# The later modulation blocks multiplied and summed on VectorE instead of TensorE, in a two-layer transformer kernel on one core

## The reference

```python
sc, scc = silu(c), silu(c_ctx)
shift, scale, gate       = split(sc  @ w_ada[l] + b_ada[l], 3)
shift_c, scale_c, gate_c = split(scc @ w_ada[l] + b_ada[l], 3)
h  = rms(x,  norm_w[l]) * (1 + scale)   + shift
hc = rms(xc, norm_w[l]) * (1 + scale_c) + shift_c
u  = h @ w_in[l]            # and hc @ w_in[l]: q, k, v of three attentions, z
x  = x + gate * ((attention outputs * silu(z)) @ w_out[l])
```

## Time and profile before

| | |
|---|---|
| median of 3 runs | 4086.47 us (4072.94 to 4087.55) |
| profiled execution, its own time | 4103.53 us |
| span in the profile | 4101.8 us |
| busy: PE, DVE, ACT, POOL | 3780.7, 1721.4, 1646.2, 67.9 us |
| mean granted TensorE clock | 0.963 of full speed |
| loaded from HBM | 570 MB, 139 GB/s over the span |

### The profile page before, as it was taken

How to read it: one execution, slowest core, us unless ns; L and a number is a source line. 1 busy time by engine, 2 the same in 40 slices (tenths; PEclk the granted TensorE clock), 3 DMA queues, 4 the chain that set the end, 5 groups by cost and what they waited for, 6 DMA issues and landing times.

```text
span 4101.8 us, 46314 instructions
## 1 busy us (share of the span) xinstructions
PE 3780.7 (92%) x19088; PEld 2938.3 (72%) x19088; DVE 1721.4 (42%) x2657; ACT 1646.2 (40%) x2577; POOL 67.9 (2%) x118
## 2 busy tenths in 40 slices
PE   7889999987989889999798999999999879999997
PEld 1557777775766657777666777776777669999886
DVE  1323444222232433443244454444554456666444
ACT  2313344443221323345444434444454554555443
POOL 1100000000010000000000000000000000000000
PEclk8899999998999999999989999999999989999999
DMA  9652221113556454222246555643645436666564
GB/s 360 173 163 67 62 57 47 46 36 97 170 174 182 136 164 134 67 79 66 56 127 197 159 160 169 189 134 112 203 147 175 134 116 188 186 186 188 175 200 149
DMA packets 350738, 577.49 MB, mean 141 GB/s; under 512 B 25268, under 2 KB 131012, under 8 KB 348352
## 3 DMA queue, kind: packets, MB, share of 16 engines
q1 hardware_dynamic: 344208, 549.47, 43.7%
q0 software_dynamic: 6320, 25.06, 2.2%
HBM read 570.26 MB, written 4.19 MB: 140 GB/s over the span
## 4 chain that ended last, share of the span: by engine, by line
PE 56%; DVE 4%; ACT 3%; DMA 1%; issue 1%; ACTq 0%; DVEq 0%
PE ps L680 35%; PE ps L1386 12%; PE ps L1107 2%; DVE w_lo L656 1%; ACT w_hi L650 1%; DMA raw_ring<-in_w_in_dram 1%; PE ps L1021 1%; PE ps L1000 1%; PE ps L1279 1%; PE ps L1286 1%; PE ps L1008 1%; ACT f_arena L1432 0%; PE ps L785 0%; PE ps L706 0%; PE ps L994 0%
## 5 line engine op out<-in xcount | busy, mean ns | idle before, releaser
L656 DVE TENSOR_TENSOR w_lo<-raw_ring,w_hi 128x1024 fp32r<-128x1024 f32 (+1 forms) x827 | 1006.2, 1223 | 1354.2 <-ACT w_hi L650 1353.2
L650 ACT CAST w_hi<-raw_ring 128x1024 fp32r<-128x1024 f32 (+1 forms) x827 | 860.7, 1047 | 1396.1 <-PE ps L680 603.6
L680 PE MATMUL ps<-w_hi,r_a 128*128 128x512 f32 x3552 | 1301.8, 407 | 102.8 <-DVE w_lo L656 36.8
L680 PE MATMUL ps<-w_lo,r_a 128*128 128x512 f32 x2624 | 1042.6, 397 | 0.0
L680 PEld LDWEIGHTS ps<-w_hi,r_a 128*128 128x128 f32 x3552 | 680.1, 191 | 331.7 <-issue 123.1
L680 PE MATMUL ps<-w_hi,r_b 128*128 128x512 f32 x2272 | 865.3, 400 | 11.4 <-DVE w_lo L656 5.5
L680 PEld LDWEIGHTS ps<-w_lo,r_a 128*128 128x128 f32 x2624 | 504.0, 192 | 106.1 <-issue 3.6
L680 PEld LDWEIGHTS ps<-w_hi,r_b 128*128 128x128 f32 x2272 | 436.6, 192 | 115.9 <-DVE w_lo L656 12.6
L1386 PE MATMUL ps<-r_a,w_hi 128*128 128x256 f32 x2816 | 499.8, 282 | 3.0 <-DVE w_lo L656 3.0
L1386 PEld LDWEIGHTS ps<-r_a,w_hi 128*128 128x128 f32 x2816 | 431.6, 189 | 3.1 <-issue 3.1
L1386 PE MATMUL ps<-r_a,w_lo 128*128 128x256 f32 x1408 | 396.6, 282 | 0.0
(11 more groups left out here) (301 smaller groups left out, 2897.7 us busy)
## 6 DMA issues: line engine op xcount, KB each, us to landing
raw_ring<-in_w_in_dram SPq DMA_DIRECT2D x386, 512.0 KB, 3.7
raw_ring<-in_ffn_w_up_dram SPq DMA_DIRECT2D x176, 512.0 KB, 4.4
raw_ring<-in_w_ada_dram SPq DMA_DIRECT2D x128, 512.0 KB, 4.4
raw_ring<-in_w_out_dram SPq DMA_DIRECT2D x96, 512.0 KB, 3.8
raw_ring<-in_ffn_w_down_dram SPq DMA_DIRECT2D x88, 512.0 KB, 3.7
gla_arena<-in_w_ada_dram SPq DMA_DIRECT2D x64, 512.0 KB, 9.0
raw_ring<-in_w_proj_b_dram SPq DMA_DIRECT2D x32, 512.0 KB, 3.7
raw_ring<-in_w_proj_a_dram SPq DMA_DIRECT2D x16, 512.0 KB, 3.7
```

Of the source, the lines that this page charges most:

```text
L650: nc.scalar.copy(WH[:, ph.s_slot(i, j), 0:n], RAW[:, ph.raw_slot(i, j), 0:n]).then_inc(hi_ready, 1)
L656: nc.vector.tensor_tensor(WL[:, ph.raw_slot(i, j), 0:n], RAW[:, ph.raw_slot(i, j), 0:n], WH[:, ph.s_slot(i, j), 0:n].bitcast(F32), ALU.sub ...
L680: mm = nc.tensor.matmul(PS[:, t, 0:cols], X(x, k, t), W[w][:, kk * cols:(kk + 1) * cols], start=(k == 0 and q == 0), stop=(c == len(js) - ...
```

## The change

The 128 later modulation chunks become a kind of their own ("M") and are no longer multiplied by TensorE. VectorE multiplies each half of a chunk (128 by 512) with the condition value of its row and adds it to an accumulator in SBUF: `dve_ada`, one instruction for each half and stream, 4 a chunk, and 2 for the four blocks of layer 1 whose context gate nobody uses (`streams`). The second half waits for the first by a semaphore. When a block's eight chunks are summed, TensorE sums over the partitions with `pe_ada_sum`: 4 products with a column of ones for each stream, 8 or 4 in place of the 4 of `pe_ada_turn`, placed in the middle of the next main chunk. The copy out of PSUM (L738) is gone, the bias stays.

The chunks are also spread anew. `PLACES` gives exactly one to each main chunk of: `win0` block 0 from chunk 2 to block 5 chunk 1; blocks 1 to 3 of `z0`; `wout0` whole; blocks 1 to 4 of `win1`. So 18 of them in layer 0, and 16 in layer 1, now lie in the attention steps. A ring slot of a modulation chunk is given back by VectorE (`mod_used`).

```diff
-        ADAW = U[0:ADAM, 0, CQ + 256:CQ + 768]
+
+        ACC = {"win": U[:, 0:2, CQ + 256:CQ + 768], "z": U[:, 2:4, CKV:CKV + NB],
+               "wout": F[:, E0 + 7168:E0 + 8192].rearrange("p (s n) -> p s n", s=2)}
...
-        HOST = {("win0", 0): ("wide", 8), ("win0", 1): ("double", 9), ("win0", 2): ("front", 11),
-                ("z0", 1): ("double", 12), ("z0", 2): ("wide", 14), ("z0", 3): ("wide", 15),
-                ("wout0", 0): ("wide", 16), ("wout0", 1): ("double", 17), ("wout0", 2): ("wide", 19),
-                ("wout0", 3): ("wide", 20), ("win1", 1): ("double", 21), ("win1", 2): ("front", 23)}
-
-        TURN = {}
-        for (name, b), (how, n) in HOST.items():
-            if how == "wide":
-                TURN[name, b + 1, 1] = n
-            else:
-                TURN[name, b, 5] = n
-                if how == "double":
-                    TURN[name, b + 1, 1] = n + 1
+        PLACES = ([("win0", 0, c) for c in range(2, 8)] + [("win0", b, c) for b in range(1, 5) for c in range(8)]
+                  + [("win0", 5, c) for c in range(2)] + [("z0", b, c) for b in range(1, 4) for c in range(8)]
+                  + [("wout0", b, c) for b in range(4) for c in range(8)]
+                  + [("win1", b, c) for b in range(1, 5) for c in range(8)])
+        HOSTED, TURN = {}, {}
+        assert len(PLACES) == 8 * len(ADAQ)
+        for k, p in enumerate(PLACES):
+            HOSTED.setdefault(p, []).append((8 + k // 8, k % 8))
+            if k % 8 == 7:
+                TURN[p] = 8 + k // 8
 
         def hosted(name, b, c):
 
-            how, n = HOST.get((name, b), ("", 0))
-            if how == "wide" and c % 2:
-                return [(n, c - 1), (n, c)]
-            if how == "double" or how == "front" and c < 4:
-                return [(n + c // 4, 2 * (c % 4)), (n + c // 4, 2 * (c % 4) + 1)]
-            return []
+            return HOSTED.get((name, b, c), [])
+
+        def turned_at(name, b, c):
+
+            return TURN.get((name, b, c - 1) if c else (name, b - 1, 7))
+
+        def streams(n):
+
+            return 1 if n >= 8 and ADAQ[n - 8][0] == 1 and ADAQ[n - 8][1] >= 8 else 2
...
-                    sp.wait_ge(pair_used if k == "S" else plain_used, n + 1)
+                    sp.wait_ge({"S": pair_used, "P": plain_used, "M": mod_used}[k], n + 1)
...
+        def pe_with_sum(pe, name, l, b, c, T):
+
+            ph, st, n = PH[f"{name}{l}"], AC[f"{name}{l}"][b], turned_at(f"{name}{l}", b, c)
+            if n is None:
+                pe_part(pe, ph, b, S8, c, 2, NB, x1, T, st, 0, T)
+            else:
+                pe_part(pe, ph, b, S8, c, 2, NB, x1, T, st, 0, T // 2)
+                pe_ada_sum(pe, n, ACC[name])
+                pe_part(pe, ph, b, S8, c, 2, NB, x1, T, st, T // 2, T)
...
+        def pe_ada_sum(pe, n, acc, to=ADAP):
+
+            pe.wait_ge(mod_used, PH[f"ada{ADAQ[n - 8][0]}"].p(n, 7) + 1)
+            for f in range(4):
+                for st in range(streams(n)):
+                    mm = nc.tensor.matmul(to[:, f, st:st + 1], acc[:, st, f * P:f * P + P], ONE,
+                                          start=True, stop=True)
+            mm.then_inc(ada_tr, 1)
+
+        def dve_ada(dve, n, ci, acc, halves=(0, 1)):
+
+            ph = PH[f"ada{ADAQ[n - 8][0]}"]
+            w = RAW[:, ph.raw_slot(n, ci)]
+            done = ph.p(n, ci)
+            for kk in halves:
+                if kk == 0:
+                    dve.wait_ge(raw_full[ph.raw_slot(n, ci)], ph.raw_full(n, ci))
+                    if ci:
+                        dve.wait_ge(mod_used, done)
+                k = 2 * ci + kk
+                for st in range(streams(n)):
+                    wk = w[:, kk * NB:(kk + 1) * NB]
+                    if k == 0:
+                        ins = nc.vector.tensor_scalar(acc[:, st, :], wk, SCT[:, k, st:st + 1], None, ALU.mult)
+                    else:
+                        ins = nc.vector.scalar_tensor_tensor(acc[:, st, :], wk, SCT[:, k, st:st + 1], acc[:, st, :],
+                                                             ALU.mult, ALU.add)
+                if kk == 0:
+                    ins.then_inc(mod_half, 1)
+                    dve.wait_ge(mod_half, done + 1)
+                else:
+                    ins.then_inc(mod_used, 1)
...
+                    halves = [(n, ci, kk) for n, ci in hosted(f"win{l}", b, c) for kk in range(2)]
+                    size = len(halves) * 2 // WT[l][b]
+                    mods[b, c, lo] = halves[size * (lo // 2):size * (lo // 2) + size]
...
-                        pe_block_part(pe, ph, b, S8, c, 2, NB, x1, range(WT[l][b]), AC[f"win{l}"][b])
-                        if (f"win{l}", b, c) in TURN:
-                            pe_ada_turn(pe, TURN[f"win{l}", b, c], ADAW)
+                        pe_with_sum(pe, "win", l, b, c, WT[l][b])
...
+                    if step in turns:
+                        pe.wait_ge(o_evac, un + before)
+                        pe_ada_sum(pe, turns[step], ACC["win"], ADAV)
                     if before is not None:
                         values(before)
...
+                def mods(name, b, c):
+
+                    n = turned_at(name, b, c)
+                    if n is not None:
+                        dve_ada_bias(dve, n)
+                    for n, ci in hosted(name, b, c):
+                        dve_ada(dve, n, ci, ACC[name[:-1]])
...
+                    mods(win, b, c)
                     rest(q + 2)
                     if c == 7 and b != 2:
...
                 def weights(name, b, c, lo, hi):
+                    if name == "win":
+                        for n, ci, kk in halves[b, c, lo]:
+                            dve_ada(dve, n, ci, ACC["win"], (kk,))
                     if name != "kt" and lo == 0:
```

More of the change, by code:

```diff
@@ L132, in build @@
         SEL = place("ada_sel", 2)
+        ONE = place("one", 1)
         NM = place("neg_max", 2)
@@ L219, in build @@
         PH, seq, kinds = {}, [], []
-        count = dict(S=0, P=0)
+        count = dict(S=0, P=0, M=0)
         def phase(name, iters, chunks):
@@ L885, in ab_parts, with ab_mods @@
             return out
+        def ab_mods(l):
+            steps, parts = ab_steps(l), ab_parts(l)
+            mods = {}
+            turns, end = {}, None
+            for k, step in enumerate(parts):
+                has = k >= 2 and steps[k - 2][0] == "s"
+                if end is not None and has:
+                    turns[k], end = end, None
+                for name, b, c, lo, hi in step:
+                    if name != "win":
+                        continue
+                    halves = [(n, ci, kk) for n, ci in hosted(f"win{l}", b, c) for kk in range(2)]
+                    size = len(halves) * 2 // WT[l][b]
+                    mods[b, c, lo] = halves[size * (lo // 2):size * (lo // 2) + size]
+                    assert not (end is not None and mods[b, c, lo]), (l, b, c)
+                    if hi == WT[l][b] and (f"win{l}", b, c) in TURN:
+                        end = TURN[f"win{l}", b, c]
+            assert end is None
+            return mods, turns
         def chain(l):
@@ L1063, in weights @@
                         pe_part(pe, PH[f"z{l}"], 0, S8, c, 2, NB, x1, T, AC[f"z{l}"][0], lo, hi)
+                turns = ab_mods(l)[1]
                 last = before = None
-                for (what, x), parts in zip(ab_steps(l), ab_parts(l)):
+                for step, ((what, x), parts) in enumerate(zip(ab_steps(l), ab_parts(l))):
                     if what == "s":
@@ L1143, in _ @@
                     for c in range(8):
[L1144 to L1148, removed]
+                        pe_with_sum(pe, "z", l, b, c, T)
                 if l == 0:
-                    pe_ada_turn(pe, 15)
+                    pe_ada_sum(pe, TURN["z0", 3, 7], ACC["z"])
                     pe.wait_ge(ada_free, 16)
@@ L1166, in _ @@
                                 pe.wait_ge(tr_free, y0 + 2)
-                            pe_block_part(pe, ph, i, S8, c, 2, NB, x1, range(4), AC["wout0"][i])
+                            pe_with_sum(pe, "wout", 0, i, c, 4)
                             if i == 0:
@@ L1173, in _ @@
                                 flip(1, c)
-                            if ("wout0", i, c) in TURN:
-                                pe_ada_turn(pe, TURN["wout0", i, c])
-                            for n, ci in hosted("wout0", i, c):
-                                pe_ada(pe, n, ci)
-                    pe_ada_turn(pe, 20)
-                    pe.wait_ge(ada_free, 21)
+                    pe_ada_sum(pe, TURN["wout0", 3, 7], ACC["wout"])
+                    pe.wait_ge(ada_free, 20)
                 else:
@@ L2185, in _ @@
                         u_sums(b)
+                if l:
+                    dve_ada_bias(dve, TURN["win1", 2, 7])
                 units, un = ab_units(l), UN[f"a{l}"]
@@ L2274, in weights @@
                             z_evac(0)
+                halves, turns = ab_mods(l)
                 last = before = None
```

(5 more changed lines are left out.)

51 lines of the change are left out of this document (18 added, 33 removed).

## The result

The changed kernel takes **4056.13 us** (median of 5 runs, 4048.44 to 4060.93) against 4080.85 for the kernel before (5 runs, 4072.94 to 4087.55): a ratio of **0.9919, 95% interval 0.9892 to 0.9946**. It is faster, by 25 us where 112 were forecast, and outside the range of 3940 to 4030. A second set of five runs on another chip gave 4048.71 against 4087.48, ratio 0.9907 [0.9892, 0.9923].

A forecast was written before the change was run, and what follows sets the result against it. The prediction took TensorE, busy 92%, as the bound, with load waits in "double" blocks. Gains of 144 less 10 for lags and 22 for attention steps made 112 us, 4086.5 to 3974 for the median, range 3940 to 4030.

The forecast's parts named there:

- attention steps: Both layers' steps with 34 hosted chunks: late loads, delayed turns and sums cost 22 us, from above 85.
- lags at flips and gates: Dense blocks: 10 us taken off the gain for lags that the 1.5 us of slack there doesn't cover.
- each new time is 8 x 5.51 = 44.1: Dense blocks: eight chunks of 24 matmuls at 0.23 us make 44.1 us, plus the boundary and the block's sum.
- the prediction's rivals: Attention steps lose much more (0.14), VectorE paces dense blocks (0.04), slower (0.04), waits not lifted (0.06), more gain (0.06).
- dense blocks: Hosting blocks of `win0`, `z0`, `wout0`, `win1`: gain 144 us together, 65 of TensorE time inside, some 79 of waits.
- "double" places: Blocks of 82.8, 67.2, 68.9 and 70.3 us, TensorE idle waiting for loads: to shrink to 48 to 55.
- The sums: TensorE's new one-column products per modulation block: 12 at 1.6 us and 4 at 0.8, 22 us in all.
- my upper bound for one sum: A sum on TensorE takes at most 3 us, with low clock and a restart of the main matmuls.
- roughly 0.7 us for two chunks: Layer 0's attention steps: TensorE's loss from turns delayed by late loads, 6 us in all.
- The large version of this rival: Attention steps lose 2 to 2.5 us a chunk, 70 to 85 in all, giving 4020 to 4046; chance 0.14.
- VectorE's price: New products take about 2.8 us a chunk, 1.4 with one stream; about 300 us more busy time, hidden behind TensorE.
- the rule of halved throughput: Rival: doubled instruction times, 5.4 us of VectorE a chunk, pace the dense blocks: 4075 to 4100; chance 0.04.

The follow-up runs named there:

- e9: e1's kernel once more, unedited, one execution: 4027.1 us, with the up projection's 256-column matmuls at 117.8 ns.
- e0: The changed kernel again, unedited, on the second chip, later tiles moved by 32 bytes: 4048.71 us against 4087.48 for the kernel before, ratio 0.9907.
- e2: The kernel before with only 32 bytes of unused space where the change has its column of ones: 4129.26 us, ratio 1.0107 to the kernel before.
- e1: The changed kernel with the column of ones in unused words of an existing tile, so nothing moves: 4001.90 us, ratio 0.9794 to the kernel before.
- e5: e1 with the 34 attention-step chunks loaded, but VectorE multiplying only 8 of 512 columns of each half: 3996.62 us, ratio 0.9778 to the kernel before.
- e6: e1 with the 34 attention-step chunks not loaded, VectorE doing all their products on a constant area: 3985.60 us, ratio 0.9745 to the kernel before.
- e8: The kernel before once more, unedited, one execution: 4083.53 us, with the up projection's 256-column matmuls at 113.3 ns.

## Why the prediction was off

Leads at the boundaries give each stage's gain. The kernel after and e9 are compared with the first profile of the kernel before; all three ran the up projection at about 118 ns:

| stage | forecast | kernel after | e9 (nothing moved) |
|---|---|---|---|
| `win0` blocks 0 to 2 | +51 | +39.3 | +39.8 |
| attention steps, layer 0 | -12 | -22.4 | -20.5 |
| per-head phase, layer 0 | 0 | -8.1 | +0.4 |
| `z0` blocks 1 to 3 | +26 | +21.8 | +22.1 |
| `wout0` | +36 | +20.0 | +22.4 |
| `win1` block 0 | 0 | +3.0 | +3.0 |
| `win1` blocks 1 and 2 | +31 | +30.7 | +30.1 |
| attention steps, layer 1 | -10 | -12.4 | -13.6 |
| per-head phase, layer 1 | 0 | -7.0 | -5.5 |
| all later work | 0 | -17.5 | -1.8 |
| lags at flips and gates | -10 | in the rows | in the rows |
| sum | +112 | +47.4 | +76.5 |

**The step that failed** is the unspoken one behind "each new time is 8 x 5.51 = 44.1" and behind everything that the sum left out: that matmuls which the change doesn't touch keep their pace. They lost 1.7% of it to the 32 bytes of the new tile. Between e0 and e9 this is 20.9 us of span. Between the kernel after and e9 it is 29.1, but 8.5 of them are the per-head phase of layer 0, which varies by execution (below); 15.7 lie in "all later work", where nothing was edited: 4704 main matmuls by 3.9 ns are 18.3. Where a stage waits for loads the slower pace costs little: e2, the kernel before shifted, loses nothing up to the end of layer 1's attention steps (0.2 us behind) and only 15.2 us in all by its profile. The cost of the shift is thus 15 to 21 us by spans. By medians it is more, 42 us between e2 and the kernel before and 47 between e0 and e1, since the unshifted kernels have executions with the better `up` pace in them and no shifted one showed it. That carries the result out of the range: on one chip the change with nothing moved gained 85.6 us by medians (e1), the change as made 38.8 (e0). None of the prediction's rivals had this mechanism in it.

It isn't the whole miss. Of the 64.6 us between 112 and 47.4, e9 accounts for 35.5 with every tile at its old address: 16.6 in the dense blocks, 12.1 in the attention steps, 5.1 in the per-head phases and 1.8 later. These terms were mis-sized, as follows.

**The dense blocks** (134 after the 10 for lags; 117.4 in e9, 114.8 in the kernel after) had the right mechanism. Main chunks in "double" places mostly run at their 5.60 us with their low part 3.0 to 3.6 us early (forecast 3.2), and 1.24 in flip and gate blocks (1.5). What was undersized is what surrounds the boundaries, and the flips (0.85 us a chunk where 0.6 was forecast). TensorE's waits at the boundary ahead of `wout0` block 3, first in the kernel before, then after; two windows of the kernel after, over the first chunk of block 2 and then over the boundary ahead of block 3; and TensorE's timeline in the first chunk of block 3:

```profile
PE ps L680 <- DVE f_arena L2358: 2.4, 1, 2.4
```

```profile
PE ps L684 <- DVE f_arena L2424: 6.1, 1, 6.1
```

```profile
1245.50:1255.70 10.20, 10.18 (x41) 8.35 (x42) 3.76 (x6) 1.05 (x1) 0.73 (x1) 0.75 0.22 84
1300.60:1307.60 7.00, 0.89 (x4) 0.09 (x2) 6.03 (x9) 1.04 (x1) 0.00 (x0) 0.84 0.52 172
```

```profile
1307.58 0.77 PE L684 MATMUL ps<-w_hi,r_a 128*128 128x512 f32 x1 [6.11 <-DVE f_arena L2424]
...
1311.56 0.63 PE L684 MATMUL ps<-w_hi,r_a 128*128 128x512 f32 x1
1311.99 0.46 PE L684 MATMUL ps<-w_lo,r_a 128*128 128x512 f32 x1
1312.29 0.40 PE L684 MATMUL ps<-w_hi,r_b 128*128 128x512 f32 x1
1312.52 1.84 PE L749 MATMUL ps<-one,f_arena 128*128 128x1 f32 x16
```

The evacuation stands behind a flip and a chunk's products on VectorE, and TensorE idles for 6.1 us instead of 2.4. Its next chunk takes 9.52 us where it was 5.60 in the kernel before. Of these 3.9 us, 2.1 are the lower clock: the first eleven matmuls are 0.43 apart (1307.58 to 1312.29) instead of 0.23. The rest is the sum of the modulation block, which stands in this chunk. The prediction priced the boundary and the sum, but slow matmuls after a pause only at the start of `win0` and of `z0`. So block 2 of `wout0` (62.1 for 56.2) is six chunks of 6.45, a first one of 10.25 and a last one, with the pause in it, of 13.13. Block 2 of `win0` (61.9 for 52.5) has a last chunk of 12.75: its boundary took 6.3 us, 4.1 of them idle, and I had costed 2.3. It also has the chunk around its sum, which follows.

**The sums** themselves were sized a little low (twelve of 1.84 to 2.38 us and four of 0.95 to 1.02, against 1.6 and 0.8). A timeline of TensorE in the kernel after, block 2 of `win0`:

```profile
236.84 0.39 PE L684 MATMUL ps<-w_hi,r_b 128*128 128x512 f32 x1
238.00 1.95 PE L749 MATMUL ps<-one,f_arena 128*128 128x1 f32 x16 [0.78 <-DVE f_arena L769]
239.81 0.48 PE L684 MATMUL ps<-w_hi,r_a 128*128 128x512 f32 x1
...
242.07 0.63 PE L684 MATMUL ps<-w_hi,r_a 128*128 128x512 f32 x1
242.50 0.63 PE L684 MATMUL ps<-w_lo,r_a 128*128 128x512 f32 x1
```

The sum is 1.95 us here, but it waits 0.78 for VectorE first, and the matmuls soon after it start 0.43 apart and not 0.23: the lower clock again. The whole chunk took 10.80 us where its neighbours with a flip took 6.45, 4.35 more, above the 3 us of my upper bound for one sum.

**The attention steps** cost 34.1 us (e9) where 22 were forecast. The mechanism was as given (late load, ScalarE and VectorE standing behind it, a delayed turn), and e5 and e6 bear it out; the size, "roughly 0.7 us for two chunks", was small. It left out that TensorE, once it idles, comes back at the lower clock, which is some 8 of the 21 us in e1. ScalarE's wait was 2.8 us a chunk. TensorE lost some 1 us a chunk of it. The large version of this rival, 70 to 85, did not come.

**VectorE's price** was right: 747 ns and 287 us in all, against the 692 to 747 ns of the earlier trace rows and "about 300". On the rule of halved throughput (the Trainium skill, "Vector Engine (DVE) Microarchitecture Reference", "Points that are easy to get wrong"), doubled times of 1.4 us don't appear: a plain `tensor_tensor` of 128x512 with two SBUF sources took 693 ns in the kernel before, the new instruction 747. This trace disagrees with the rule as I had applied it.

**Left open.** By what path an address that is no multiple of 64 bytes slows a matmul, and which of the moved tiles does it, wasn't tried. Nor was what sets the up projection's pace at its start. Shifting by 64 gives 227 to 230 ns for 512 columns and 120.0 for 256, so 64-byte alignment isn't the whole rule. The per-head phase of layer 0 lost 8.1 us in the kernel after, but also in e8, the unedited kernel before, and none in e9: it varies by execution, and I put no cause to it.

The best version is e1, the change with nothing moved: 2.1% faster than the kernel before by its median of four (a later single execution, e9, 1.5% below the one of the kernel before beside it, 4087.03 us), where the change as made is 0.8 to 0.9%.

## What to carry to other kernels

A new tile, however small, is a change to every tile behind it: before a sum of times is trusted, list which addresses move, and compare the pitch of matmuls that nobody edited. Hidden work on an in-order engine is hidden only while that engine's other inputs are early; here 18 chunks of products, some 50 us, cost nothing that could be seen while the loads were early, and about 10 us more than the late loads did alone. And spacing can be worth more than placement on an engine: the same products, two chunks at a time, made the kernel 1.6% slower. After a pause of TensorE, count the matmuls that follow it at the lower clock as well as the pause.

## What the runs showed of the hardware that I hadn't expected

- Matmuls of 512 columns start 229 ns apart with the tiles at their old addresses, 233.3 with all later tiles moved by 32 bytes, and 227 to 230 moved by 64, at granted clock 1.00 and with TensorE busy throughout in each.
- Matmuls of 256 columns in the up projection run at 113.3 or 117.8 ns in different executions of one kernel at the same addresses, without a change from the stage's start to its end, 19 us in all; at 118.3 when moved by 32 bytes and at 120.0 when moved by 64.
- After a TensorE pause of 6.1 us, and after one of 3.6 us, the next eleven and twelve matmuls of 512 columns started 0.43 us apart, at the lower of the two clocks, 1.2 GHz, and not 0.23: 2.1 and 2.4 us lost after the pause. A wait of 0.78 us with a sum of one-column products behind it (238.00 above) was followed by such a stretch too.
